# A mixture of 16,384 experts on one core: a group of four blocks that still lacks its product with u is put ahead of the twenty kept groups

## The reference

```python
def one(xb):                                  # h: (tokens, 1024)
    ...                                       # scores, two rounds of top-16 -> eid, softmax g
    ug = jnp.take(u_tab, eid, axis=0)         # u_tab, v_tab: (16384, 1024)
    vg = jnp.take(v_tab, eid, axis=0)
    act = jax.nn.gelu(jnp.einsum('td,thkd->thk', xb, ug).astype(F32))
    return jnp.einsum('thk,thkd->td', (g * act).astype(xb.dtype), vg)
```

## Time and profile before

| | |
|---|---|
| device time, median of 3 runs | 5075.16 us (5073.82 to 5082.77) |
| the profiled execution, its own time | 5069.28 us |
| span of its trace | 5067.6 us |
| busy in the span: PE, PE weight loads, DVE, ACT, POOL | 88%, 45%, 47%, 22%, 19% |
| mean granted TensorE clock | 0.94 |
| units of the second pass (L2640, 6656 matmuls) | 379 ns each, pipelined |
| products with u (L2599, 9216 matmuls) | 318 ns each, pipelined |

### The profile page before, as it was taken

The page is one execution under the profiler, slowest core; times in us unless marked ns, Lnnn a source line. Parts: engine busy times, 40 slices in busy tenths (PEclk is TensorE's granted clock), DMA queues, the critical chain, the costliest instruction groups (busy, mean ns, idle before and its releaser), DMA issues. The chain is left out here.

```text
span 5067.6 us, 67239 instructions
## 1 busy us (share of the span) xinstructions
PE 4449.0 (88%) x26722; PEld 2305.7 (45%) x26722; DVE 2393.8 (47%) x4394; ACT 1124.5 (22%) x1398; POOL 980.8 (19%) x551
## 2 busy tenths in 40 slices
PE   4998865698674989999999969999999999999993
PEld 3674431355433534555555534444444444444441
DVE  4232114566434205888888735555554332332324
ACT  4232112233322112333333310001001111111113
POOL 0000000222001000000000035555554222222220
PEclk8999877899796999999999989999999999999997
DMA  5332344321453125789966676677675444444432
GB/s 171 101 106 85 104 103 167 95 83 63 144 174 108 67 72 153 250 238 280 281 194 199 203 183 143 143 151 147 144 148 116 98 96 92 100 100 88 100 68 81
DMA packets 1025827, 688.92 MB, mean 136 GB/s; under 512 B 847026, under 2 KB 922890, under 8 KB 1017355
## 3 DMA queue, kind: packets, MB, share of 16 engines
q1 hardware_dynamic: 1013716, 591.63, 46.0%
q10 hardware_dynamic: 4896, 71.31, 3.4%
q0 software_dynamic: 6976, 22.55, 1.2%
HBM read 442.99 MB, written 205.97 MB: 128 GB/s over the span
## 5 line engine op out<-in xcount | busy, mean ns | idle before, releaser
L2640 PE MATMUL ex_psy<-ex_vhi,ex_wboth 128*128 128x512 f16 x4352 | 1322.3, 379 | 41.8 <-issue 41.8
L2640 PE MATMUL ex_psy<-ex_vlo,ex_wboth 128*128 128x512 f16 x2304 | 874.0, 379 | 0.0
L2330 POOL TENSOR_SCALAR ex_v<-ex_v 128x1024 f32<-128x1024 f32 x128 | 396.7, 3099 | 2322.7 <-DMA ex_v<-in_peer_v_dram 2322.3
L2599 PE MATMUL ex_psa<-h_hi,ex_uth 128*128 128x512 f16 (+1 forms) x3072 | 641.2, 318 | 73.7 <-ACT ex_wa L2355 50.1
L2640 PEld LDWEIGHTS ex_psy<-ex_vhi,ex_wboth 128*128 128x128 f16 x4352 | 426.0, 98 | 556.6 <-issue 43.8
L2599 PE MATMUL ex_psa<-h_lo,ex_uth 128*128 128x512 f16 (+1 forms) x3072 | 641.8, 318 | 0.0
L2599 PE MATMUL ex_psa<-h_hi,ex_utl 128*128 128x512 f16 (+1 forms) x3072 | 641.6, 318 | 0.0
L2581 DVE TENSOR_TENSOR ex_acc<-ex_acc,ex_psy 128x512 f32<-128x512 f32 x558 | 372.4, 683 | 477.3 <-PE ex_psy L2640 476.9
L2570 DVE SCALAR_TENSOR_TENSOR ex_wa<-ex_wa,ex_gate 128x1088 f32<-128x1088 f32 x128 | 201.3, 1572 | 532.2 <-ACT ex_wa L2355 503.9
L2355 ACT ACTIVATE ex_wa<-ex_psa 128x1088 f32<-128x1088 f32 x128 | 137.9, 1077 | 1206.6 <-PE ex_psa L2599 1206.5
L2599 PEld LDWEIGHTS ex_psa<-h_hi,ex_uth 128*128 128x128 f16 x3072 | 234.6, 98 | 320.2 <-issue 69.6
(11 more groups left out here) (365 smaller groups left out, 5678.8 us busy)
## 6 DMA issues: line engine op xcount, KB each, us to landing
gate_all<-rt_stage ACTq DMA_DIRECT2D x34, 2048.0 KB, 6.7
ex_gate<-gate_all SPq DMA_DIRECT2D x128, 544.0 KB
ex_u<-in_peer_u_dram SPq DMA_DIRECT2D x128, 512.0 KB, 5.2
ex_v<-in_peer_v_dram SPq DMA_DIRECT2D x128, 512.0 KB, 8.1
act_all<-ex_wa SPq DMA_DIRECT2D x80, 544.0 KB, 3.5
ex_wa<-act_all SPq DMA_DIRECT2D x80, 544.0 KB, 3.8
ad_w<-in_ada_w_dram SPq DMA_DIRECT2D x8, 2048.0 KB, 8.0
pa_w<-in_w_in_dram SPq DMA_DIRECT2D x10, 1024.0 KB, 7.9
```

Source lines behind the costliest of these rows:

```text
L2330: nc.gpsimd.tensor_scalar(v[s][:, :], v[s][:, :], SPLIT, None, ALU.mult).then_inc(v_sc, 1)
L2599: mm = nc.tensor.matmul(ps_a[:, c:e], x[s][:, k, :], h[:, k, c:e], start=(k == 0 and j == 0), stop=(k == KD - 1 and j == len(mms) - 1))
L2640: mm = nc.tensor.matmul(ps_y[n % YB][:, :], w, v_[:, a * 512:(a + 1) * 512], start=(j == 0), stop=(j == len(mms) - 1))
```

## The change

The order of the second pass becomes: group 20 first (blocks 80 to 83, not kept), then the twenty kept groups 0 to 19, then groups 21 to 31. Since blocks no longer stand in the order of their numbers, waits count places (`n`), and `block_at` says which block stands at a place. SP's wait for all stores of `wa` moves from ahead of the second pass to the first kept block; ACT waits for the last store of each `wa` buffer before it writes a gelu there. Two more groups are written out straight, and the loop over groups that are not kept has four rounds instead of five.

```diff
                 half(0, None, 0)
-                half(1, 0, 1)
+                half(1, 0, 1, True)
                 with eng.Fori(1, FIRST // 2) as i:
                     half(i * 2, i * 2 - 1, 0, True)
                     half(i * 2 + 1, i * 2, 1, True)
-                with eng.Fori(FIRST // 2, NGR // 2 - 1) as i:
+                half(FIRST, FIRST - 1, 0, True)
+                half(FIRST + 1, FIRST, 1)
+                with eng.Fori(FIRST // 2 + 1, NGR // 2 - 1) as i:
                     half(i * 2, i * 2 - 1, 0)
                     half(i * 2 + 1, i * 2, 1)
...
-            def is_kept(g1, kept):
-                return kept or (isinstance(g1, int) and g1 < FIRST)
+            def block_at(g1, b, kept):
+
+                if isinstance(g1, int) and g1 == 0:
+                    return AHEAD + b
+                return g1 * EB + b - EB if kept else g1 * EB + b
...
-                for s in range(2):
-                    sp.wait_ge(wa_stored[s], AHEAD // 2 * 16)
                 sp.wait_ge(routed, PT + 1)
...
-                        eb, s = g1 * EB + b, b % 2
-                        if is_kept(g1, kept):
-                            sp.wait_ge(w_lo_done, eb + 1)
+                        n, eb, s = g1 * EB + b, block_at(g1, b, kept), b % 2
+                        if kept:
+                            if isinstance(g1, int) and n == EB:
+                                sp.wait_ge(wa_stored[0], AHEAD // 2 * 16)
+                                sp.wait_ge(wa_stored[1], AHEAD // 2 * 16)
+                            sp.wait_ge(w_lo_done, n + 1)
                             sp.dma_start(wa[s][:, :], act_all[eb]).then_inc(wa_in[s], 16)
...
-                            act.wait_ge(w_lo_done, eb + 1)
+                            if isinstance(g1, int) and n < 2:
+                                act.wait_ge(wa_stored[s], AHEAD // 2 * 16)
+                            act.wait_ge(w_lo_done, n + 1)
                             gelu(eb, s)
...
-                        if g1 is not None and not is_kept(g1, kept):
-                            eb = g1 * EB + b
+                        if g1 is not None and not kept:
+                            eb = block_at(g1, b, kept)
                             products(eb, b % 2, range(KD))
```

More of the change, by code:

```diff
@@ L2311, in half @@
                             sp.wait_ge(stage_stored[1], (PT * 2 + 1) * 16)
-                        sp.wait_ge(w_done, eb + 1)
+                        sp.wait_ge(w_done, n + 1)
                         sp.dma_start(gate[s][:, :].rearrange("p (m t) -> p m t", t=RUN), gates[eb]).then_inc(g_in[s], 16)
-                        sp.wait_ge(v_lo_done, eb + 1)
+                        sp.wait_ge(v_lo_done, n + 1)
                         sp.dma_start(v[s][:, :], rows_of("peer_v", eb)).then_inc(v_in[s], 16)
@@ L2401, in half @@
                     for b in range(EB) if g1 is not None else ():
-                        eb, s, k = g1 * EB + b, b % 2, EB * p + b
-                        if not is_kept(g1, kept):
+                        n, eb, s, k = g1 * EB + b, block_at(g1, b, kept), b % 2, EB * p + b
+                        if not kept:
                             if more(eb, 2):
                                 split(eb + 2, s)
-                            act.wait_ge(w_lo_done, eb + 1)
+                            if isinstance(g1, int) and n < 2:
+                                act.wait_ge(wa_stored[s], AHEAD // 2 * 16)
+                            act.wait_ge(w_lo_done, n + 1)
                             gelu(eb, s)
-                        act.wait_ge(w_done, eb + 3)
+                        act.wait_ge(w_done, n + 3)
                         if not (isinstance(g1, int) and g1 < 2):
@@ L2561, in half @@
                         if g1 is not None:
-                            eb, s, k = g1 * EB + b, b % 2, EB * p + b
-                            if is_kept(g1, kept):
+                            at, eb, s, k = g1 * EB + b, block_at(g1, b, kept), b % 2, EB * p + b
+                            if kept:
                                 dve.wait_ge(wa_in[s], (eb - s) * 8 + 16)
@@ L2568, in half @@
                                 dve.wait_ge(gelu_done, eb + 2)
-                            dve.wait_ge(g_in[s], (eb - s) * 8 + 16)
+                            dve.wait_ge(g_in[s], (at - s) * 8 + 16)
                             V.scalar_tensor_tensor(wa[s][:, :], wa[s][:, :], WSCALE, gate[s][:, :], ALU.mult, ALU.mult).then_inc(w_done, 1)
-                            dve.wait_ge(w_hi_done, eb + 1)
+                            dve.wait_ge(w_hi_done, at + 1)
                             V.tensor_tensor(w_both[k][:, TOK + NS:], wa[s][:, 0:SEQ], w_both[k][:, 0:SEQ], ALU.subtract)
```

## The result

The changed kernel took 5051.18 us (median of five runs, 5048.94 to 5052.89), the kernel before 5075.16 (five runs, 5073.71 to 5082.77): 24.0 us less, ratio 0.9949 with a 95% interval of 0.9935 to 0.9964. A second comparison gave 0.9945 (0.993 to 0.9961).

What follows compares the result with a forecast made beforehand. PE was taken to bound all three regimes; 44.59 us of products moved into its wait, less a 15.35 us later start, gave 29.2 us off, 5075.2 to 5046 us, with a range of 5037 to 5058.

Steps and rivals of the forecast that it cites:

- The hole and its filling: Seam between the passes: PE idles 41.84 us while POOL splits four blocks; 288 matmuls fill it, 12.54 us a block.
- The later start: First unit after the seam starts at 3029.8 instead of 3014.45, 15.35 us later; the mark is block 79's gelu start.
- v chain: Seam, block 83: transposes' issue to POOL's start on v 12.29 us, then POOL 6.29; ends 3028.90, up to 3029.87.
- w chain: Seam, block 83: gelu 1.08 us, DVE's gate product 1.29 to 3.20, subtractions 2.54; ends 3027.77 or 3029.68.
- The clock: PE's half rate after the seam's idle: same 1.7 us loss as before; bounds a gain of 1.7, a loss of 0.9.
- the loop over not-kept groups has one round less, which is within this mean: Not-kept groups: 89.49 us each against 44.90 kept, so 44.59 us saved, with no separate charge for the loop.
- slow seam: Rival, chance 0.14: transfers pace the seam at 14.0 us a block, start 7.4 us later, gain 22, time 5053.
- The chains: Rival, chance 0.05: at the seam, gates and v flow only after the products; start 50.2 us later, time 5081.
- Kept groups: Rival, chance 0.05: their preparation, with 4.8 us of cover, falls behind; 8 us longer in each gives 5110.
- expected signs: Profile: PE's hole 6 to 8 us, seam blocks 12.5 each, first unit near 3029.8, kept groups 44.9, not-kept 89.5.

Runs made afterwards that it cites:

- e4: Changed kernel with SP's transposes of block 84 issued behind the gate and v of block 83 instead of ahead of them; 5041.68 us, one run.
- e1: Changed kernel with the loop over not-kept groups 22 to 29 written out straight; 5042.6 us, median.
- e2: Changed kernel with 32 empty instructions at PE's start in the expert stage, so later PE code stands further on; 5043.03 us, median.
- e3: Kernel before the change with 202 empty instructions at PE's start in the expert stage, putting its not-kept loop where the changed kernel has it; 5099.12 us, one run.

## Why the prediction was right, and where not

- **The hole and its filling: right.** PE's wait was the wait for group 0's preparation, and 288 matmuls went into it at 12.55 us a block (forecast 12.54).
- **The later start: right in the sum, partly by luck.** Forecast 57.1 us after the mark, measured 57.65 and 58.29. The v chain ended 0.3 us and the w chain 0.6 us behind the later of the two ends forecast for each. But I charged DVE's gate product 3.20 us while POOL works, and it took 1.35; from its end to the end of the last subtraction it took 4.94 us instead of 2.54. The two errors nearly cancel. The 3.20 was measured beside POOL's last operation on v (from 3012.29 and 3012.22 on); here the product met POOL's first (3028.34 to 3031.11), and the last subtraction met POOL's last. With v earlier, e4 shortens what follows the gelu by 1.6 us.
- **The clock: within the bounds.** The windows above say that it fell just ahead of 3033 and rose at 3039.8 (0.61 over that us), 4.3 us after PE came back: 2.1 us lost against 1.7 before. I took no difference.
- **The step that failed** is the sentence that "the loop over not-kept groups has one round less, which is within this mean". I took the back edges as part of an unchanging mean. There were fewer, but the code in front had grown, and each cost 2.0 to 2.6 us instead of 0.7 to 0.9. These 4.0 us are most of the 5.0 by which the gain fell short of 29.2 in the trace. The rest is the later start (0.55), the clock (0.4) and the part of a back edge in the mean of 89.49 (0.35), less the 0.3 behind the last unit. e1 takes the back edges away, e2 takes away the 4.0 by moving code alone, and e3 brings the dearer back edges into the kernel before.
- **The rivals.** The slow seam did not come: a block took 12.55 us and not the rival's 14.0, with 128-byte gates and all. The chains did not wait for the products. Kept groups stayed at 44.89 us with no wait of PE among them. The expected signs came true, but for the not-kept groups' 89.5 us at the back edges.
- **The range.** Its bounds, gains of 17 and 38 us, do not come out of the figures that the prediction gives for them: 22 − 7.6 is 14.4, and 32.9 + 1.3 is 34.2. The measured 24.0 lies within either pair.

## What to carry to other kernels

Where the bound engine waits for a pipeline to fill, put work there that it must do anyway and whose own inputs are already at hand; it is worth its bound time less what the fill is delayed, and one more piece behind it can cover the rest. Lay executions side by side from a mark ahead of the change, since everything before it adds its own scatter. And when a change adds straight code ahead of a loop, look at the loop's back edges on the bound engine, and at the packets of its code, even if its body is the same.

## What the runs showed of the hardware

- A back edge of the loop over not-kept groups (2038 PE instructions a round) cost 0.7 to 0.9 us on PE where the loop stood in the kernel before, and 1.95 to 2.83 us in the changed kernel and e3, where it stood 202 instructions further on (modulo 256, counted in the built program with a weight load per matmul). The loop over kept groups (874 instructions a round) showed no wait, and in the changed kernel no packet of code from 3162 to 3903. The Trainium skill, "Runtime: NRT & Kernel Launch", Instruction fetch mechanics, says that code comes in blocks of 256 instructions and that a taken branch out of what is loaded has to fetch its target first. The trace agrees: each of these waits on PE ends 1.2 to 1.8 us after a packet of 16 KiB on the instruction queue, the second wait comes always after the same eight matmuls, and it goes when the code is moved by 32. That the eight matmuls end where a block ends is argued, not seen.
- DVE's subtraction on 64 columns took 0.21 us, and 2.14 beside POOL's last operation on v (3022.03 and 3033.31 above). The Trainium skill, "SBUF — State Buffer", Who interferes with whom, says that DVE with two inputs in SBUF and a GpSimd operation that reads SBUF share a port pair, and that the later one blocks until the other is done. The trace agrees there: POOL's operation from 3032.40 ends at 3035.37, DVE's from 3033.31 at 3035.45. It does not agree for POOL's first operation on v: in e4 the same subtraction, from 3027.79, took 0.21 us while POOL was at it from 3025.76 to 3028.53. What makes the difference is open.
